# Retention decay tables made head by head, three loads on ScalarE's queue, and the plain gate blocks split between front and end

## What is computed

```python
def retention_mixer(a_ctx, a_lat, w_in, decay_param, w_out, want_ctx):
    log_gamma = -jnp.exp(decay_param.astype(jnp.float32))     # (2 directions, 4 heads)
    def project(a, rope):
        q, k, v, g = jnp.split(a @ w_in, ...)                  # 4 heads; dk 256, dv 512
        if rope is not None:
            q, k = apply_rope(q, *rope), apply_rope(k, *rope)
        k = k * RET_DK ** -0.5
        ...
    o_ctx, o_lat = bidirectional_scan(ctx_terms, lat_terms)    # S_t = gamma S_{t-1} + k_t v_t, both ways
    def readout(o, g):
        y = rms_norm_2(o)...
        return (jax.nn.silu(g) * y) @ w_out
```

## Time and profile before

| what | value |
|---|---|
| median of 3 runs | 2966.15 us (2964.76 to 2968.64) |
| the profiled execution | 2970.24 us |
| its span, first to last instruction | 2968.4 us |
| TensorE busy, of the span | 2782.5 us (94%) |
| VectorE, ScalarE, GpSimd busy | 2023.3 us (68%), 1283.5 us (43%), 369.4 us (12%) |
| mean granted TensorE clock | 0.971 |

### The profile page before, as it was taken

How to read it: one execution, slowest core, us unless ns; L and a number is a source line. 1 busy time by engine, 2 the same in 40 slices (tenths; PEclk the granted TensorE clock), 3 DMA queues, 4 the chain that set the end, 5 groups by cost and what they waited for, 6 DMA issues and landing times.

```text
span 2968.4 us, 42896 instructions
## 1 busy us (share of the span) xinstructions
PE 2782.5 (94%) x16374; PEld 2488.8 (84%) x16374; DVE 2023.3 (68%) x3722; ACT 1283.5 (43%) x2369; POOL 369.4 (12%) x207
## 2 busy tenths in 40 slices
PE   9999999999999399989997899999989998999998
PEld 8888987988888298978886889999977777989898
DVE  7788688769878567744546687666674435677676
ACT  5322357633235444432223634334446435554354
POOL 2243200124330000011110000000002222000000
PEclk9999999999999699999998999999989999999999
DMA  6556321256552333323321012222222121122322
GB/s 198 192 182 198 121 95 50 84 190 202 184 161 67 135 137 142 116 104 131 131 96 50 16 59 71 70 71 65 80 71 75 47 72 49 65 79 72 114 86 79
DMA packets 99613, 312.19 MB, mean 105 GB/s; under 512 B 10320, under 2 KB 25808, under 8 KB 97872
## 3 DMA queue, kind: packets, MB, share of 16 engines
q1 hardware_dynamic: 92208, 287.42, 29.7%
q10 hardware_dynamic: 7200, 22.02, 2.0%
HBM read 283.71 MB, written 24.12 MB: 104 GB/s over the span
## 4 chain that ended last, share of the span: by engine, by line
PE 51%; DVE 6%; ACT 2%; issue 1%; DMA 1%; POOL 0%; DVEq 0%; ACTq 0%; SPq 0%; POOLq 0%
PE ps L2248 16%; PE ps L2249 16%; PE ps L2250 16%; DVE t_wlo L2974 1%; PE ps L2531 1%; PE ps L2515 1%; PE ps L2504 1%; ACT t_whi L2574 1%; DVE t_x L3208 0%; DVE t_m L3208 0%; DVE t_m L3093 0%; DMA t_m<-s_dec 0%; DMA t_raw<-in_gu 0%; DVE t_x L3174 0%; DVE t_h L3214 0%
## 5 line engine op out<-in xcount | busy, mean ns | idle before, releaser
L2574 ACT CAST t_whi<-t_raw 128x512 fp32r<-128x512 f32 (+3 forms) x494 | 381.4, 783 | 671.5 <-PE ps L2250 457.4
L2248 PE MATMUL ps<-t_h,t_whi 128*128 128x256 f32 (+2 forms) x1852 | 628.3, 339 | 7.7 <-DVE t_wlo L2974 2.6
L2249 PE MATMUL ps<-t_h,t_wlo 128*128 128x256 f32 (+2 forms) x1852 | 623.6, 337 | 0.0
L2250 PE MATMUL ps<-t_h,t_whi 128*128 128x256 f32 (+2 forms) x1852 | 623.6, 337 | 0.0
L2974 DVE TENSOR_TENSOR t_wlo<-t_raw,t_whi 128x512 fp32r<-128x512 f32 (+3 forms) x420 | 356.9, 861 | 121.2 <-ACT t_whi L2574 116.7
L2248 PEld LDWEIGHTS ps<-t_h,t_whi 128*128 128x128 f32 x1852 | 354.7, 192 | 42.2 <-issue 9.9
L2249 PEld LDWEIGHTS ps<-t_h,t_wlo 128*128 128x128 f32 x1852 | 354.8, 192 | 26.1 <-issue 0.2
L2250 PEld LDWEIGHTS ps<-t_h,t_whi 128*128 128x128 f32 x1852 | 354.6, 191 | 26.3
L2248 PE MATMUL ps<-t_mw,t_whi 128*128 128x256 f32 (+2 forms) x922 | 299.3, 325 | 74.6 <-ACT t_tmp L2579 34.8
L2248 PE MATMUL ps<-t_hid,t_whi 128*128 128x256 f32 (+2 forms) x1032 | 335.5, 325 | 0.7 <-DVE t_hid L3273 0.6
L2249 PE MATMUL ps<-t_hid,t_wlo 128*128 128x256 f32 (+2 forms) x1032 | 333.6, 323 | 0.0
(11 more groups left out here) (373 smaller groups left out, 4962.5 us busy)
## 6 DMA issues: line engine op xcount, KB each, us to landing
t_raw<-in_gu SPq DMA_DIRECT2D x174, 512.0 KB, 3.4
t_raw<-in_ada SPq DMA_DIRECT2D x96, 512.0 KB, 3.6
t_raw<-in_dn SPq DMA_DIRECT2D x52, 512.0 KB, 4.2
t_raw<-in_dn SPq DMA_DIRECT2D x24, 384.0 KB, 3.4
s_qk<-t_hid ACTq DMA_DIRECT2D x12, 768.0 KB, 4.3
t_hid<-s_qk SPq DMA_DIRECT2D x6, 1536.0 KB, 11.6
t_raw<-in_ret_v SPq DMA_DIRECT2D x16, 512.0 KB, 4.8
t_raw<-in_ret_g SPq DMA_DIRECT2D x16, 512.0 KB, 3.8
```

Of the source, the lines that this page charges most:

```text
L2248: e.matmul(out, whi, xlo, start=first, stop=False, skip_group_check=shared)
L2249: e.matmul(out, wlo, xhi, start=False, stop=False, skip_group_check=shared)
L2250: return e.matmul(out, whi, xhi, start=False, stop=last, skip_group_check=shared)
L2574: e.copy(m.block(0, it.slot, n), m.raw(it)).then_inc(*S["hi"].of(j))
```

## The change

1. **Decay tables.** The table of each head is computed in place, in the memory where `ret_score` reads it, just before that head's attention: a 768 KB load of distances (`dist_load`), two VectorE operations, one add, three exponentials and two adds (`ret_decay`). Head 0's is put between the last q/k pair and the last gate pair, those of heads 1 to 3 behind the attention of the head before. The stores to HBM and the loads back are gone, and so is the wait of the rotation table for the last decay table.
2. **Queues.** `dist_load`, `rope_load` and `v_load` are issued on ScalarE's queue and not on SyncE's.
3. **Gates.** One plain block (head 3, c 2) stands in front instead of two; the pair list starts with (1, 0) and leaves out (3, 1), so it is still 7 pairs; the other plain block (head 3, c 3, `late_gate`) stands behind the attention of the last head, context columns first, with its Silu written straight to where `ret_y` reads it.
4. **Planner.** A transfer over 1024 columns is planned longer by 1.3 ns a column, and the point from which the planner puts heads first is ScalarE's `ret_setup`.

```diff
-        def decays(h, after):
-            put("ret_decay", h=h, after=after, slot=[e for k in range(4) for e in slots.get(("b", k), [])])
-            free([("b", k) for k in range(4)], ("ret_gs", h))
-            put("dec_store", h=h)
-            return [("d_ds", h)]
...
-        def plain_gates(h, i):
+        def early_gate(h, c):
...
+        def late_gate(h, c, after):
+            def post(g):
+                put("g_late", h=h, c=c, g=g.id, bank=g.bank, t0=g.t0, n=g.n, after=after)
+            columns([(("ret_g", h * 4 + c), (SLOT,), DC, ("h", 4), [(0, "drain_act", post)])], SEG2[::-1])
...
                 if (t0, i) == (0, 1):
                     finish(h, 512, 256)
-                    gated_values(h, 512, 256)
+                    gated_values(h, 512, 256, range(4 if h < n_head - 1 else 3))
+            if h == n_head - 1:
+                from_bank(4)
+                late_gate(h, 3, ov["oc"])
+                gated_values(h, 512, 256, (3,))
             finish(h, 0, 512)
-            gated_values(h, 0, 512)
+            gated_values(h, 0, 512, range(4))
...
-        put("ret_setup", after=pro + state["hid_free"])
+        put("ret_setup", after=pro)
         token_sums("ret", 4, 384, pro)
         last_sums("ret", 4, 384, pro)
-        late = pro
-        for h in range(n_head):
-            late = decays(h, late)
-        put("rope_load", after=[("ret_act", ("ll", n_head - 1))])
-        sides[:] = [late] * 4
-        plain_gates(1, 0)
+        put("rope_load", after=pro)
+        sides[:] = [pro] * 4
+        early_gate(n_head - 1, 2)
...
-        gate_pairs = [(1, 1), (2, 0), (2, 1), (3, 0), (3, 1), (0, 0), (0, 1)]
+        gate_pairs = [(1, 0), (1, 1), (2, 0), (2, 1), (3, 0), (0, 0), (0, 1)]
         pairs = [(h, w) for h in (1, 2, 3, 0) for w in range(2)]
         for k, (h, w) in enumerate(pairs):
             seven_pair("qk", h, w)
+            if k == len(pairs) - 1:
+                rope_done = sides[0] + sides[1] + sides[2] + sides[3]
+                put("dist_load", h=0, after=rope_done)
+                put("ret_decay", h=0, after=rope_done)
             if k != 3:
                 last = seven_pair("g", *gate_pairs[k - (k > 3)])
...
-        put("dec_load", h=0, after=rope_done + [("d_ds", n_head - 1)])
         put("v_load", after=[("ps", last["P6"])])
...
             attend(h)
+            if h < n_head - 1:
+                put("dist_load", h=h + 1, after=[("drain_dve", ("ret_p", h, 0, 5))])
+                put("ret_decay", h=h + 1, after=[("p_lo", (h, 0, 5))])
...
-                put("dec_load", h=h + 1, after=[("drain_dve", ("ret_p", h, 0, 5))])
...
     def ret_decay(it):
-        h, d2 = it.h, m.LRU[:, 7168:7808]
-        ll, gs, ta, tb = m.at(RTAB, 896), m.at(RTAB + 896, 640), m.at(RTA, 896), m.tmp(1024, 896)
+        h = it.h
+        ll, gs, tb = m.at(RST, 896), m.at(RST + 896, 640), m.at(RPA, 896)
         w.wait_ge("ret_dve", ("d3", h))
         wait_all(it.after)
-        e.activation(ll, ta, ACT.Exp).then_inc(*S["ret_act"].of(("ll", h)))
+        e.activation(ll, ll, ACT.Exp).then_inc(*S["ret_act"].of(("ll", h)))
         yield
-        e.activation(gs, d2, ACT.Exp, scale=m.sm(8 + h, 1)).then_inc(*S["ret_act"].of(("g1", h)))
-        e.activation(tb[:, 0:640], d2, ACT.Exp, scale=m.sm(4 + h, 1), bias=m.sm(20 + h, 1)).then_inc(*S["ret_act"].of(("g2", h)))
+        e.activation(tb[:, 0:640], gs, ACT.Exp, scale=m.sm(4 + h, 1), bias=m.sm(20 + h, 1)).then_inc(*S["ret_act"].of(("g2", h)))
+        w.wait_ge("ret_act", ("g2", h))
+        e.activation(gs, gs, ACT.Exp, scale=m.sm(8 + h, 1)).then_inc(*S["ret_act"].of(("g1", h)))
```

More of the change, by code:

```diff
@@ L319, in arrange @@
                     end = op.due
-        self.heads_on = next(op.item.id for op in self.ops["sync"] if op.item.kind == "ret_setup")
+        self.heads_on = next(op.item.id for op in self.ops["scalar"] if op.item.kind == "ret_setup")
         return self.run(families)
@@ L1516, in finish, with gated_values @@
             put("ret_recip", h=h, t0=t0, n=n)
-        def gated_values(h, t0, n):
-            for c in range(4):
+        def gated_values(h, t0, n, some):
+            for c in some:
                 put("ret_y", h=h, c=c, t0=t0, n=n)
@@ L2813, in ret_decay, with dist_load, v_load, rope_load @@
     def ret_decay(it):
[L2814 to L2815 removed]
+        h = it.h
+        ll, gs, tb = m.at(RST, 896), m.at(RST + 896, 640), m.at(RPA, 896)
         w.wait_ge("ret_dve", ("d3", h))
         wait_all(it.after)
[L2818 removed]
+        e.activation(ll, ll, ACT.Exp).then_inc(*S["ret_act"].of(("ll", h)))
         yield
[L2820 to L2826 removed]
+        e.activation(tb[:, 0:640], gs, ACT.Exp, scale=m.sm(4 + h, 1), bias=m.sm(20 + h, 1)).then_inc(*S["ret_act"].of(("g2", h)))
+        w.wait_ge("ret_act", ("g2", h))
+        e.activation(gs, gs, ACT.Exp, scale=m.sm(8 + h, 1)).then_inc(*S["ret_act"].of(("g1", h)))
+    def dist_load(it):
+        wait_all(it.after)
+        e.dma_start(m.at(RST, 1536), dram["dist"]).then_inc(*S["d_dist"].of(it.h))
+    def v_load(it):
+        wait_all(it.after)
+        w.wait_ge("d_vs0", 0)
+        for part in range(2):
+            o, src = (RVV, RVL)[part], dram["s_v"][part]
+            e.dma_start(m.MW[:, o + 2048:o + 3072].bitcast(F32), src[:, 2048:3072]).then_inc(*S["d_rv0"].of(("part", part), 0))
+        for part in range(2):
+            o, src = (RVV, RVL)[part], dram["s_v"][part]
+            e.dma_start(m.MW[:, o:o + 2048].bitcast(F32), src[:, 0:2048]).then_inc(*S["d_rv1"].of(("part", part), 0))
+    def rope_load(it):
+        wait_all(it.after)
+        e.dma_start(m.at(RCS, 1024), dram["rope"]).then_inc(*S["d_ret"].of("rope"))
     def v_store(it):
@@ L2857, in g_last, with g_late @@
         e.activation(m.tmp(it.off, it.n), m.PS[:, it.bank, 0:it.n], ACT.Silu).then_inc(*S["drain_act"].of(it.key, ("g", it.h, it.c, it.half)))
+    def g_late(it):
+        w.wait_ge("ps", it.g)
+        wait_all(it.after)
+        e.activation(m.ret_gate(it.c, it.t0, it.n), m.PS[:, it.bank, 0:it.n], ACT.Silu).then_inc(*S["drain_act"].of(it.g, ("g_late", it.t0)))
     def g_silu(it):
```

83 lines of the change are left out of this document (31 added, 52 removed).

## The result

The changed kernel takes **2770.03 us** (median of 4 runs, 2769.56 to 2771.22) against 2967.19 us of the kernel before in the same session: a ratio of 0.9337, 95% interval 0.9321 to 0.9353. That is 197 us faster, where 77 were forecast; the measured time lies 100 us under the range. Something large was not in the sum.

A forecast was written before the change was run, and what follows sets the result against it. TensorE, busy 94%, bounds the kernel; gain could only come from its 186 us idle and lower-clock products. Terms −57 − 10 + 0 − 10 = −77 took 2970.2 to 2893, as a median 2889 us; range 2880 to 2899, with rivals 2870 to 2910.

The forecast's parts named there:

- Front: Front of retention: without tables and 24 `t_x` operations there, the next pair begins near 982, not 1038.9: −57 us.
- Start of attention: First weighted score: the table, made in place, is ready before TensorE asks, so its 8.4 us wait goes: −10 us.
- Heads: Between heads: three tables are covered by idle VectorE and ScalarE and by the next head's products: 0 us.
- Behind the last head: After the last head: late gate costs 8.3 us, y comes earlier, the rest to FFN3 is bound by VectorE: −10 us.
- the sum of −77: Whole kernel: front −57, start of attention −10, heads 0, behind the last head −10.
- (e): Rival on ScalarE's table loads: each of 11 more switches holds up TensorE, 14 us in all, 2903 us; chance 0.04.

The follow-up runs named there:

- e1: Kernel before, retention unchanged; the planner's pass lets go of SyncE's written order when stuck, so all 22438 rows get due times: 2807.64 us, ratio 0.9465.
- e2: Changed kernel with one never-met need on a weight load, so only 7261 of 22430 rows get a due time by propagation: 2927.22 us, ratio 0.9866.
- e7: Changed kernel with the three transfers (distances, rotation table, values of head 0) back on SyncE's queue: 2778.57 us, ratio 0.9369.
- e4: Changed kernel with both plain gate blocks in front and none behind the last head: 2768.12 us, ratio 0.9331.
- e10: The kernel of e4 (changed kernel, both plain gate blocks in front) again, five rounds: 2768.89 us, ratio 0.9327.
- e6: Kernel before, due times still lost; rows with equal due times spaced the other way, first listed due first: 2861.52 us, ratio 0.9646.
- e5: Kernel before with its own order up to neighbourhood attention, and from there on the order of e1: 2913.22 us, ratio 0.9822.

## Why the prediction was wrong

1. **The failed step** is one that the text made without saying so. It worked out retention only and put 0 on the rest. The total that it started from, "the 186 us in which TensorE is idle" and "products that run at the lower clock", was right (151 and 49 us of it were gained), but I looked for it only at the items that the diff touches. The order of every row is the planner's result. Between the kernel before and e1, which have the same rows, the traces differ at 648 of 16374 places of TensorE's order, but at 2019 of 3722 of VectorE's and 1704 of 2369 of ScalarE's; TensorE's order alone made the rest look unchanged. e1 measures what that left out: 159 us.
2. **Front, "−57 us".** Right: −62.2, and TensorE's pair begins 63.5 us earlier, 3 of it brought along. The two causes that the text names are both real, the tables and ScalarE's order ahead of the copies. But the second doesn't come from the edits. e1 gains 29.6 with all four tables still in front; e2, with the tables gone and due times lost, gains 30.2 beside the 8.3 of the block, and keeps a wait of 25.9 us. In it stand the T casts, the DMA issues and the 24 operations on `t_x`, which take 7.45 us; e1, with due times, runs those in the pairs, from 1130 on.
3. **Start of attention, "−10 us".** Right in size: −9.1, with the table ready before TensorE asks. The reason was half of it: with the table made in place but due times lost (e2) the stage gains nothing, and with due times alone (e1) 1.3. And e7 shows that 8.7 us hang on the three transfers being on ScalarE's queue.
4. **Heads, "0 us".** Right, −0.7, with TensorE 99.6% busy.
5. **Behind the last head, "−10 us", "bound by VectorE".** Here a step that was worked out failed. The latent part of `ret_o` starts 21.8 us after the last value product (1525.6 − 1503.8), where the text expected 24 to 25 and 34.8 was before: so 13 us and not 10, about as forecast. The other 24 us of the 37 came after that, where the text had 0, since VectorE's 54.2 us of work in 66 were taken as work that had to be done before FFN3. With due times part of it, casts and sums for later, stands behind what TensorE needs. And the 10 us didn't come from the edits either: with the edits alone (e2) the stage is 0.6 us longer, with due times alone (e1) 40.5 shorter. In e2 a wait of 8.6 us for the low part of weights stands within the context part of `ret_o`. The late gate, which I had made the cause, is not one (e4, e10).

   So of the sum of −77, the edits as such are worth 39 us: the front's term for the greater part, the other two hardly at all. The terms of 2, 3 and 5 were read from an order of rows that had its due times, and came out for that reason.
6. **Table loads.** (e) falls: of TensorE's waits behind the start none is over 1.4 us, and heads with three tables between them are no longer than before, so nothing shows the 14 us. ScalarE in the changed kernel, where it goes back from the exponentials to Silu:

```profile
1183.06 1.04 ACT L2558 CAST t_whi<-t_raw 128x1024 fp32r<-128x1024 f32 x1
1184.12 1.28 ACT L2855 ACT_TABLE_LOAD   x1
1185.41 0.49 ACT L2855 ACTIVATE t_tmp<-ps 128x384 f32<-128x384 f32 x1
```

   The load starts 0.02 us behind the end of the cast (1184.10), and the Silu 0.01 us behind the load. The Trainium skill, ScalarE: Activation LUTs, section "What ACT_TABLE_LOAD costs", puts a drain of about 1.38 us on top of the load; these rows show room for it on neither side, and the switch costs 1.31 us in all.

What stays open: why e6 leaves the front's wait of 28.5 us and the last 300 us as they were was not tried. Nor was the share of the clock told apart: the 49 us of shorter busy time come with the waits, and no run had one without the other. They aren't a fixed share of the waits, though: e5 and e2 are idle for 147 and 150 us, and busy for 30 and 43 us more than the changed kernel.

## What to carry to other kernels

When a planner or scheduler writes the order, a diff's reach is the whole program: compare each engine's order, not only TensorE's, before any stage gets a 0. Waits of a few us for many different results, spread over stages with idle VectorE and ScalarE (here 18 us for one cast in 6 waits, 31 us for layer norms in 12), were here the mark of an order without priorities, and worth more than the one large hole beside them. And a planner's pass over a graph should say when it ends with rows left: here the pass never reached 15,151 of 22,438 rows, which left 4,325 without a due time, and a fallback of eight lines on the old kernel was worth 159 us, four times what all the edits of the kernel were.

## What the runs showed of the hardware

In the changed kernel the granted clock stays at its upper level, 2.4 GHz, from its first record at 6.1 us until behind the last product (0.999 on average against 0.971), though 35 us of idle time are left in it, in waits of up to 3.0 us, none over 1.4 us behind the start. The same 16374 matmuls then take 2733.4 us of busy time instead of 2782.5. In this kernel, waits that are that short cost only themselves; in the kernel before, 186 us of waits came with 49 us of longer products.

The length of a single wait doesn't tell whether the clock falls. In e4 one of 1.99 us ends at 1511.47, and the records have the lower level from 1511.4 to 1514.8; in e2 one of 2.24 us ends at 1041.34, and the clock stays at the upper level from 992.2 to 1227.7.
